# A hybrid decoder layer on one NeuronCore: table products on VectorE, a first weight tile by halves, state products in another order, and a store from another queue

## What is computed

```
h = rms_norm(x, g_mix)
z = h @ w_in            # q, k, v of 3 dilation groups (3 x 512 columns each), u (512), gate_a, gate_s (1024 each)
a = dilated_attention(q, k, v) @ w_attn_proj
y = gelu(s5_ssm(u))     # 32 groups x 64 complex states, 16 channels a group
s = (y @ w_glu_a) * sigmoid(y @ w_glu_b)
x = x + (sigmoid(gate_a) * a + sigmoid(gate_s) * s) @ w_out
h2 = rms_norm(x, g_ffn)
x = x + (silu(h2 @ w_ffn_gate) * (h2 @ w_ffn_up)) @ w_ffn_down
...
# the state space part: per group a diagonal recurrence x_t = A x_(t-1) + B u_t, y_t = Re(C x_t) + D u_t
abar = exp(lambda * dt);  bbar = (abar - 1) / lambda * b
```

## Time and profile before

| | us |
|---|---|
| median of three runs | 887.63 |
| the three runs | 884.7, 887.63, 887.9 |
| the profiled execution | 885.96 |
| its span | 884.1 |
| TensorE busy in it | 864.8 (98%) |
| VectorE, ScalarE, GpSimd busy | 439.0, 322.8, 190.0 |

### The profile page before, as it was taken

One profiled execution on the slowest core, in us unless ns is written; L12 is line 12 of the kernel. 1 busy time (PEld: TensorE's weight loads), 2 busy tenths in 40 slices (PEclk: granted clock), 3 DMA queues, 4 the chain that ended last, 5 costly groups with the idle time before them and its releaser, 6 DMA issues.

```text
span 884.1 us, 13117 instructions
## 1 busy us (share of the span) xinstructions
PE 864.8 (98%) x4601; PEld 712.2 (81%) x4601; DVE 439.0 (50%) x625; ACT 322.8 (37%) x486; POOL 190.0 (21%) x219
## 2 busy tenths in 40 slices
PE   5999999999999999999999999999999999999998
PEld 4888888888887877877887888888888888888886
DVE  5553475687924444444587554333333334433334
ACT  6312343323235656656433343222222222322221
POOL 3699988850020000001220220000000000000000
PEclk9999999999999999999999999999999999999999
DMA  7429334474365552413545232333333332222222
GB/s 278 143 83 250 96 121 143 154 172 166 115 188 157 173 150 81 141 50 94 140 145 185 81 102 90 97 98 101 101 100 97 95 95 96 96 95 95 95 71 96
DMA packets 85938, 108.82 MB, mean 123 GB/s; under 512 B 10672, under 2 KB 51872, under 8 KB 85776
## 3 DMA queue, kind: packets, MB, share of 16 engines
q1 hardware_dynamic: 80096, 96.34, 34.7%
q10 hardware_dynamic: 4400, 8.42, 3.2%
q0 software_dynamic: 1408, 3.61, 2.0%
HBM read 94.38 MB, written 13.96 MB: 123 GB/s over the span
## 4 chain that ended last, share of the span: by engine, by line
PE 53%; DVE 2%; issue 0%; ACT 0%; DVEq 0%; ACTq 0%
PE ps L1430 27%; PE ps L1460 13%; PE ps L1179 12%; DVE late L1161 1%; DVE late L1081 0%; DVE hT_lo L1087 0%; PE ps L1349 0%; PE ps L1335 0%; DVE w_lo L556 0%; ACT w_hi L550 0%; PE ps L1445 0%; DVE late L1084 0%; PE ps L1440 0%; PE ps L1325 0%; DVE late L1012 0%
## 5 line engine op out<-in xcount | busy, mean ns | idle before, releaser
L556 DVE TENSOR_TENSOR w_lo<-w_raw,w_hi 128x1024 fp32r<-128x1024 f32 x142 | 186.0, 1310 | 332.3 <-ACT w_hi L550 332.2
L550 ACT ACTIVATE w_hi<-w_raw 128x1024 fp32r<-128x1024 f32 x142 | 150.4, 1059 | 396.7 <-PE ps L1179 162.6
L1430 PE MATMUL ps<-h_hi,w_hi 128*128 128x512 f32 x352 | 137.2, 390 | 0.0
L1430 PE MATMUL ps<-h_hi,w_lo 128*128 128x512 f32 x352 | 137.0, 389 | 0.0
L1430 PE MATMUL ps<-h_lo,w_hi 128*128 128x512 f32 x352 | 136.9, 389 | 0.0
L407 POOL TENSOR_TENSOR early<-early 128x16 f32<-128x16 f32 (+8 forms) x141 | 128.4, 911 | 23.4 <-ACT early L573 12.4
L1179 PE MATMUL ps<-w_hi,hT_hi 128*128 128x512 f32 x288 | 113.4, 394 | 10.5 <-DVE w_lo L556 10.3
L1179 PE MATMUL ps<-w_hi,hT_lo 128*128 128x512 f32 x288 | 112.7, 391 | 0.0
L1179 PE MATMUL ps<-w_lo,hT_hi 128*128 128x512 f32 x288 | 112.6, 391 | 0.0
L1179 PE MATMUL ps<-hT_hi,w_hi 128*128 128x512 f32 x224 | 91.5, 408 | 0.0
L1179 PE MATMUL ps<-hT_hi,w_lo 128*128 128x512 f32 x224 | 87.7, 391 | 0.0
(11 more groups left out here) (200 smaller groups left out, 1054.6 us busy)
## 6 DMA issues: line engine op xcount, KB each, us to landing
...
```

The lines of the kernel that those rows point to most:

```text
L550: nc.scalar.activation(w_hi[:, j % WSPL], w_raw[:, j % WRAW], ACT.Copy).then_inc(w_hi_done, 1)
L556: nc.vector.tensor_tensor(w_lo[:, j % WSPL], w_raw[:, j % WRAW], w_hi[:, j % WSPL].bitcast(F32), ALU.subtract).then_inc(w_lo_done, 1)
L1430: ins = T.matmul(ps[:, m], (w_hi, w_lo)[b][:, j % WSPL, at_w:at_w + P], (h2_hi, h2_lo)[a][:, 2 * j + h, :], start=j == 0 and h == 0 and k ...
```

## The change

- GpSimd no longer makes `aB` and `ca`. VectorE makes the same 12 products, one or two at a time between the `lo` of W_V1 and of the first two chunks (`table_steps`), each waiting for the one before it. TensorE waits for all 12 before it turns `aB`.
- x is loaded in five pieces (1, 1, 2, 2, 2 tiles). The first two weight tiles are loaded from ScalarE's queue, ahead of its own work. The first weight tile is rounded, subtracted and multiplied by halves of 128 rows, in the order of the operands. A one-column ACTIVATE stands ahead of the first wait for data. TensorE begins with 13 products of `ones`, whose result nobody reads.
- `squares` of the second half comes after `hi` of the third tile; `hi` of the fourth tile and of W_U's first comes earlier on ScalarE, `lo` of the fourth tile earlier on VectorE. The squares are summed on TensorE one step later, and the norm is spread after two steps of W_U instead of before them.
- The state products: quarters of pairs 0 to 3, whole ones of pairs 8 to 11, quarters of pairs 4 to 7, whole ones of pairs 12 to 15, then all the products with `toep`.
- The last value chunk is stored from ScalarE's queue right after its last move out of PSUM, on a semaphore of its own; SP waits for that one.

```diff
+WARM = 13
+X_PIECES = ((0, 1), (1, 2), (2, 4), (4, 6), (6, 8))
...
-            for j in range(4):
-                sp.dma_start(xt[:, 2 * j:2 * j + 2], t["xt"][:, 2 * j:2 * j + 2]).then_inc(xt_loaded[j], 16)
-                load(W_V0 + j, j, in_cols(6))
+            for n, (k, k_end) in enumerate(X_PIECES):
+                if n == 3:
+                    sp.wait_ge(raw_landed[0], 16)
+                if n == 4:
+                    load(W_V0 + 2, 2, in_cols(6))
+                sp.dma_start(xt[:, k:k_end], t["xt"][:, k:k_end]).then_inc(xt_loaded[n], 16)
+            load(W_V0 + 3, 3, in_cols(6))
...
-            sp.wait_ge(act_evac, AE_Z)
-            sp.wait_ge(dve_evac, DE_Z)
-            store_z(sp, 8, 0)
-            sp.wait_ge(z_stored, 16 * 9)
+            sp.wait_ge(last_z_stored, 16)
             load_values(0)
             sp.wait_ge(y_stored, 16 * CL)
...
-            cmul(aB[:, 0], aB[:, 1], for_k(apw[:, 0], CL), for_k(apw[:, 1], CL),
-                 for_c(bb[:, 0, 0:NPR], CL), for_c(bb[:, 1, 0:NPR], CL), tmp(CL))
-
-            pool.wait_ge(misc_act, MA_C)
-            cmul(ca[:, 0], ca[:, 1], for_k(apw[:, 0], CL + 1), for_k(apn, CL + 1),
-                 for_c(ctr[:, 0], CL + 1), for_c(ctr[:, 1], CL + 1), tmp(CL + 1))
+            TAB["powers"] = n_tab[0]
+
...
+            def gained(k):
+                nc.scalar.activation(hT_hi[:, k], xt[:, k], ACT.Copy, scale=gmixT[:, k:k + 1]).then_inc(hT_hi_done, 1)
+
+            for j in range(2):
+                for h in range(2):
+                    act.dma_start(w_raw[:, j, h * 512:(h + 1) * 512], in_cols(6)(j, h)
+                                  ).then_inc(raw_landed[j] if j or h else raw_first, 16)
+            act.wait_ge(pool_tab, 1)
+            nc.scalar.activation(zsq[:, 0:1], minus_half[:, 0:1], ACT.Copy)
             act.wait_ge(gains_in, 16)
-            for j in range(4):
-                act.wait_ge(xt_loaded[j], 16)
-                for k in (2 * j, 2 * j + 1):
-                    nc.scalar.activation(hT_hi[:, k], xt[:, k], ACT.Copy, scale=gmixT[:, k:k + 1]).then_inc(hT_hi_done, 1)
-                if j < 2:
-                    hi(W_V0 + j, j)
-                if j % 2:
-                    squares(j // 2)
-
-            hi(W_V0 + 2, 2)
+            for h in range(2):
+                act.wait_ge(xt_loaded[h], 16)
+                gained(h)
+                act.wait_ge(raw_landed[0] if h else raw_first, 16)
+                nc.scalar.activation(w_hi[:, 0, h * 512:(h + 1) * 512], w_raw[:, 0, h * 512:(h + 1) * 512], ACT.Copy
+                                     ).then_inc(w_hi_done if h else w_hi_first, 1)
+            for n in range(2, 5):
+                act.wait_ge(xt_loaded[n], 16)
+                for k in range(*X_PIECES[n]):
+                    gained(k)
+                if n != 3:
+                    hi(W_V0 + n // 2, n // 2)
+                if n > 2:
+                    squares(n - 3)
+
             act.wait_ge(params_in, PARAMS)
             nc.scalar.activation(sv[DT], sv[DT], ACT.Exp).then_inc(act_tab, 1)
+            hi(W_V0 + 3, 3)
             act.wait_ge(dve_tab, 2)
             nc.scalar.activation(sv[MAG], sv[ZR], ACT.Exp).then_inc(act_tab, 1)
             nc.scalar.activation(sv[M8], sv[ZR], ACT.Exp, scale=float(CL)).then_inc(act_tab, 1)
-            hi(W_V0 + 3, 3)
+            hi(W_U, 0)
             act.wait_ge(dve_tab, 10)
             nc.scalar.activation(sv[SIN], sv[RR], ACT.Sin).then_inc(act_tab, 1)
             nc.scalar.activation(sv[S2], sv[RR], ACT.Sin, scale=0.5).then_inc(act_tab, 1)
-            hi(W_U, 0)
...
+            act.wait_ge(act_evac, AE_Z)
+            act.wait_ge(dve_evac, DE_Z)
+            act.dma_start(z_d[8].rearrange("(m p) c -> p m c", p=P), zs[:, 0]).then_inc(last_z_stored, 16)
...
+            def gained_lo(k):
+                dve.wait_ge(hT_hi_done, k + 1)
+                V.scalar_tensor_tensor(out=hT_lo[:, k], in0=xt[:, k], scalar=gmixT[:, k:k + 1],
+                                       in1=hT_hi[:, k].bitcast(F32), op0=ALU.mult, op1=ALU.subtract).then_inc(hT_lo_done, 1)
+
+            for h in range(2):
+                gained_lo(h)
+                dve.wait_ge(w_hi_done if h else w_hi_first, 1)
+                V.tensor_tensor(w_lo[:, 0, h * 512:(h + 1) * 512], w_raw[:, 0, h * 512:(h + 1) * 512],
+                                w_hi[:, 0, h * 512:(h + 1) * 512].bitcast(F32), ALU.subtract
+                                ).then_inc(w_lo_done if h else w_lo_first, 1)
+            for j in range(1, 4):
                 for k in (2 * j, 2 * j + 1):
-                    dve.wait_ge(hT_hi_done, k + 1)
-                    V.scalar_tensor_tensor(out=hT_lo[:, k], in0=xt[:, k], scalar=gmixT[:, k:k + 1],
-                                           in1=hT_hi[:, k].bitcast(F32), op0=ALU.mult, op1=ALU.subtract
-                                           ).then_inc(hT_lo_done, 1)
+                    gained_lo(k)
                 if j < 3:
                     lo(W_V0 + j, j)
+            lo(W_V0 + 3, 3)
             dve.wait_ge(act_tab, 1)
             tab(V.tensor_tensor(sv[ANG], sv[LI], sv[DT], ALU.mult))
             tab(V.tensor_tensor(sv[ZR], sv[LR], sv[DT], ALU.mult))
-            lo(W_V0 + 3, 3)

             tab(V.tensor_scalar(sv[KQ], sv[ANG], 1.0 / TWO_PI, ROUND, ALU.mult, ALU.add))
...
+            lo(W_U, 0)
...
+            lo(W_U + 1, 1)
...
+            def table_products():
+
+                n_prod = [0]
+                for_k = lambda a, n: a[:, 0:n, :].rearrange("p k q -> p q k").unsqueeze(3).to_broadcast([P, NPR, n, CH])
+                for_c = lambda a, n: a.unsqueeze(2).to_broadcast([P, NPR, n, CH])
+
+                def prod(out, a, b, op):
+                    if n_prod[0]:
+                        dve.wait_ge(table_prods, n_prod[0])
+                    n_prod[0] += 1
+                    V.tensor_tensor(out, a, b, op).then_inc(table_prods, 1)
+
+                dve.wait_ge(pool_tab, TAB["powers"])
+                for n, out, im, b_re, b_im in ((CL, aB, apw[:, 1], bb[:, 0, 0:NPR], bb[:, 1, 0:NPR]),
+                                               (CL + 1, ca, apn, ctr[:, 0], ctr[:, 1])):
+                    if n > CL:
+                        dve.wait_ge(misc_act, MA_C)
...
+                    for step in ((out[:, 0], re, b_re, ALU.mult), (tmp, im, b_im, ALU.mult),
+                                 (out[:, 0], out[:, 0], tmp, ALU.subtract), (out[:, 1], re, b_im, ALU.mult),
+                                 (tmp, im, b_re, ALU.mult), (out[:, 1], out[:, 1], tmp, ALU.add)):
+                        prod(*step)
+                        yield
+
+            products = table_products()
+
+            def table_steps(n):
+                for _ in range(n):
+                    next(products)
+
             for j in range(2, 5):
                 lo(W_V1 + j, j)
+                table_steps(1)
...
-            z_chunk(0, True)
-            z_chunk(1)
+            z_chunk(0, True, tables=(2, 1, 2, 1))
+            z_chunk(1, tables=(2, 0, 0, 1))
...
+            pe.wait_ge(pool_tab, 2)
+            for _ in range(WARM):
+                T.matmul(ps[:, 7, 0:P], ones[:, :], ones[:, :], start=True, stop=True)
+            for h in range(2):
+                for k, (a, b) in enumerate(((0, 0), (1, 0), (0, 1))):
+                    if k == 0:
+                        pe.wait_ge(hT_hi_done, h + 1)
+                        pe.wait_ge(w_hi_done if h else w_hi_first, 1)
+                    elif k == 1:
+                        pe.wait_ge(hT_lo_done, h + 1)
+                    else:
+                        pe.wait_ge(w_lo_done if h else w_lo_first, 1)
+                    for m in range(4):
+                        ins = T.matmul(ps[:, m], h_acts[a][:, h, m * P:(m + 1) * P], (w_hi, w_lo)[b][:, 0, h * 512:(h + 1) * 512],
+                                       start=h == 0 and k == 0, stop=False)
+                        if h and k == 2:
+                            ins.then_inc(gemm_steps, 1)
+
+            def rest_of_first():
+                for j in range(1, 4):
+                    yield from products(W_V0 + j, j, False, j == 3, by_token(h_acts, j), None, lambda m: gained_rows(j, m))
+
+            v0 = rest_of_first()
+            for _ in range(10):
                 next(v0)
             pe.wait_ge(sq_sum, 1)
             for n in range(TB):
                 ins = T.matmul(ps[:, 6, 2 * n:2 * n + 2], sq[:, n * P:(n + 1) * P], ones[:, 0:2], start=True, stop=True)
             ins.then_inc(norm_sums, 1)
             run(v0)
+            def sums_read(m):
+                if m >= 2:
+                    pe.wait_ge(norm_eps, m - 1)
+            u_in = columns(W_U, 4, by_feature, h_acts, sums_read, None, 4)
+            for _ in range(2):
+                next(u_in)
             pe.wait_ge(ident_in, 16)
             pe.wait_ge(norm_done, 1)
             for n in range(TB):
```

(31 more changed lines are left out.)

27 lines of the change are left out of this document (15 added, 12 removed).

## The result

The changed kernel takes **880.92 us** (median of 5 runs, 880.65 to 881.24); the kernel before, in the runs beside it, 887.63 (884.7 to 887.9). The ratio is 0.994, with a 95% interval from 0.9925 to 0.9956, about 5 us. Runs of the kernel before that were made beside the experiments (57 of them) have medians of 886.15, 886.30 and 886.21; measured from there the gain is 5.3 us. The forecast was 882.0, in a range from 879.0 to 886.5. Total and direction came out as forecast. Of the terms in the sum, the first tile was too small, the one for the state products had the wrong cause, and the one for the values was far too small, as the experiments show.

The account below looks back on a forecast made before the run. TensorE, busy 98% of the span, was taken as the bound, so its waits and slow stretches decide: 2.3 - 0.1 (norm moves) - 0.2 + 1.5 + 1.1 = 4.6 us off a level of 886.6 gives 882.0, range 879.0 to 886.5.

Parts of the forecast that it names:

- the first tile: Start of TensorE: first product earlier, fourth weight tile at 26.1 instead of 28.4, a gain of 2.3 us.
- the state products: Pause of 1.5 us among them: instruction supply falls behind the densest stretch; the new order spreads it, gain 1.5 us.
- the values: Last value chunk: its store leaves earlier from ScalarE, value loads start some 6 us earlier, TensorE's wait goes, gain 1.1 us.
- TensorE's side: Start: first product near 6.5 instead of 10.3; idle products take 3.3 to 6.7 us; 5.6 us won at TensorE.
- the supply: ScalarE and VectorE at the start: third tile rounded at 17.2, subtracted by 19.9; fourth ready at 26.1.
- the reason named: Fourth weight tile: VectorE, slowed beside GpSimd's sums, delivers at 26.1, while TensorE could take it at 25.3.
- The table products: VectorE in W_V1 and the first chunks: 2.35 to 2.6 us each, no gain, 0.2 us lost to small waits.
- one of the places worked out: Between a chunk's last `lo` and the moves out of PSUM: 3.7 us for the product, nothing shows at 2.35 to 2.6.
- The slower rival: Table products make VectorE the bound, as slow as GpSimd: 15 us lost, 897; chance 0.06.
- At 4.6 us after its start, when the supply had delivered 154 before, it asks for 147: State products: the new order asks for fewer products than the supply had delivered by then, so no pause, 1.5 us.
- the signs that I had named: First product at 6 to 7.5, fourth tile about 26, `w_lo` waits before third and fourth, shorter pause, products 2.3 to 3.0.
- The signs of being wrong: TensorE waits for VectorE inside chunks, fourth tile begins before 25 or after 27.5, or the state-product pause stays.

Follow-up runs that it names:

- a_nosums: Changed kernel without GpSimd's sums of squares (four of five additions left out, the last cut to 16 columns; norm not computed): 880.63 us, in two heaps.
- a_warm0: Changed kernel without the idle products (`WARM = 0`): 881.37 us.
- b_store: Kernel before with only the last value chunk's store moved to ScalarE's queue: 885.55 us, ratio 1.0001.
- b_first: Kernel before with the first tile by halves, its new loads and the moves around the norm, without idle products: 883.40 us, ratio 0.9973.
- b_order: Kernel before with only the new order of the state products: 888.12 us, ratio 1.0016.
- b_warm: Kernel before with only the 13 idle products ahead of the first product: 890.06 us, ratio 1.0047.
- a_oldorder: Changed kernel with the old order of the state products: 880.89 us.
- b_store_shift: Kernel before with the last store on ScalarE's queue and 108 already-met waits (54 instructions) ahead of TensorE's first product: 882.52 us, ratio 0.996.
- a_best2: Changed kernel with weight tiles two to four term by term, W_U's first subtraction earlier, one table product moved to W_V1, old state-product order: 880.28 us.
- a_pool: Changed kernel with the twelve table products back on GpSimd: 881.02 us.
- a_best: Changed kernel with weight tiles two to four term by term and the first chunk's last table product moved into the second chunk: 880.99 us.
- a_spstore: Changed kernel with the last value chunk stored from SP's queue again: 884.91 us.

## Why the prediction was right, and where it was not

**The sum** had 4.6 us; the two traces differ by 5.1, the times by 5.3. It came out because one term that was too small met another that had the wrong cause and, by luck, the right size.

**The first tile: right in kind, too small.** Forecast 2.3, measured 3.85 at the fourth weight tile. TensorE's side was right (6.48 for 6.5; the idle products, priced at 3.3 to 6.7, took 5.1, and the clock was up before the first real product). The step that was off is the supply: I had the third tile ready at 19.9, with 2.71 for its subtraction, as beside GpSimd in the earlier trace rows. It was ready at 17.7: ScalarE's chain ran 0.9 us earlier than summed (its rounding ended at 16.26 for 17.2), and the subtraction took 1.44, though the sums had begun. TensorE did not wait there. The fourth tile did wait for the reason named, 0.97 for 0.8, and VectorE's pair took 4.58, not 3.48; a_nosums confirms the cause. That the supply has slack to swallow shows in a_warm0: of 2.5 us by which the second tile is late, 1.2 are left at the fourth. The "GPSIMD Engine Reference" of the Trainium skill, section "Specifications", names this contention, and these runs agree with it (1.23 alone, 4.68 at worst), but the slowing is nothing to be priced by one row: 1.44 to 4.68 for the same instruction.

**The table products: right that they win nothing.** Forecast -0.2. In the trace they cost 0.68 and a slower restart, at one of the places worked out (the product ahead of the moves: 1.48 + 2.76 + 0.74 against a limit with 3.7 for the product); that slot was tighter than reckoned since the subtraction ahead of it ended late, behind two products of 2.7 each. Back on GpSimd they cost as much in another place, by the contention. The slower rival did not occur: a product took 2.3 to 2.8.

**The state products: the size was right, the cause was wrong.** Forecast 1.5, measured 1.34, but not by the order: without it the time is 880.89. The step that failed is "At 4.6 us after its start, when the supply had delivered 154 before, it asks for 147". The pause stands at a place in the program, not at a density. Before, b_store, b_first and b_order have it after 154 products, that is 308 instructions with the weight loads, in either order. Move TensorE's program by 54 instructions (52 in b_warm) and it is gone (b_warm, a_oldorder, b_store_shift, a_best2), and where the new order still shows one, it is after 255 products or 510 instructions: 308 - 54 + 256. The page "Runtime: NRT & Kernel Launch" of the Trainium skill, section "Instruction fetch mechanics", has instructions come in blocks of 256 and their crossing mostly hidden; the distance agrees, the hiding depends. In before the packet for the next block comes at 244.24, 2.3 us after the stage began; in a_oldorder the one for the block whose border lies after 127 products comes at 237.00, 2.6 us **before** the stage, while TensorE is still at wide products. In the eight kernels with a pause (before, b_order, b_store, b_first, after, a_pool, a_nosums, a_best) it ended 2.25 to 2.38 us after the last such packet ahead of it. (The records do not name the engine that a packet is for; that these are TensorE's blocks is read from this spacing.) It is not enough to ask whether the packet falls into the dense stretch: in a_warm0 it comes at 243.22, 3.1 us into the stage, and the first product behind the border starts 2.32 us after it, held up by 0.13; in a_spstore it comes 4.5 us into the stage and 4.5 ahead of that product, which is not held up at all. So in these traces the product behind the border never starts less than 2.25 us after the packet, and the pause is what is missing to that. A dense stretch reaches the border sooner, which leaves less time. My text had said that the idle products' instructions "shift everything behind them, which can help or hurt here", and gave it neither a price nor a chance. That was the rival to work out. What sets the moment of the packet stays open: with the same program order and borders it came 7.1 us after the stage's start in after and 4.5 in a_spstore, and of the two only after has a pause.

**The values: right in kind, far too small, and not a term of its own.** Forecast 1.1, which the trace shows. But with the store put back on SP's queue the changed kernel is 4.0 us slower, and moved to ScalarE's in the old kernel it wins 0.7 by the medians, which is not clear of noise. Two steps failed. First, terms were added that lean on each other: what any change ahead of pair 0 wins without moving the last chunk comes back as a wait for the values (1.07 in before, 3.31 in b_order), and with the earlier store the pause was longer (1.50 in before, 2.76 in b_store), which fits that the store's data are then in the DMAs' way, though that is not shown. Second, a wait was priced at its own length. With waits of 2.02, 2.76, 3.31 and 3.68 us the granted clock went to half for 3.4 or 6.8 us; with those of 1.07 and 1.50 it did not. So the values' wait and the pause are two gates in a row, and the two opened together give 3.7 us, more than the 2.6 I had for the two.

**The sum by parts, as the runs give it:** the first tile 2.8 (b_first), idle products 0.45 more (in the traces 1.2 at the fourth tile, of which the pause takes 0.4 back), store and shift together 3.7 (b_store_shift), order 0, table products 0. That is 7 by parts for 5.3 in all; the rest is not accounted for by a run of its own, but the trace of after shows what the parts alone did not have: the wait of 0.68 with its restart, the pause of 0.35 and 0.3 more in the wait for ScalarE's copies.

**What would show it:** of the signs that I had named, the fourth tile at "about 26" came at 24.5, and the wait for `w_lo` before the third tile did not come; no wait for `late<-z_d`, a shorter "issue" row and products at 2.3 to 3.0 did. The signs of being wrong fared worse: the fourth tile began before 25, TensorE did wait for VectorE inside the first chunk (0.68), and the pause stayed, though at 0.35 and at another place. By these signs the path was wrong in three places while the total was right.
